# One whole load of the output projection's weights, shared by prompt and sample, in the attention kernel of a hybrid decoder layer

## The reference

```python
q, k, v (two head groups) = rms_norm(x) @ w_in          # 1024 -> 3072
oa = (softmax(q1 k1') - lam * softmax(q2 k2')) v        # 4 heads, 128-wide; sample: over 32 cache pages of 128 keys
oa = rms_norm(oa per head) * (1 - lambda_init)
ob = three dilated windows, combined                    # 8 heads, 64-wide; sample: over a 2048-row state
x  = x + concat(oa, ob) @ w_out                         # 1024 x 1024, for the prompt AND for the samples
x  = x + (silu(h @ w_gate) * (h @ w_up)) @ w_down       # h = rms_norm(x), 1024 -> 2816 -> 1024
y  = rms_norm(x)
```

## Time and profile before

| | us |
|---|---|
| median of 3 runs | 1243.67 (1239.3 to 1248.49) |
| the profiled execution | 1240.77 |
| its span, first to last instruction | 1238.9 |
| PE busy in it | 1020.4 (82%) |
| DVE busy | 564.7 (46%) |
| ACT busy | 419.4 (34%) |
| POOL busy | 249.4 (20%) |

### The profile page before, as it was taken

How to read it: one execution, slowest core, us unless ns; L and a number is a source line. 1 busy time by engine, 2 the same in 40 slices (tenths; PEclk the granted TensorE clock), 3 DMA queues, 4 the chain that set the end, 5 groups by cost and what they waited for, 6 DMA issues and landing times.

```text
span 1238.9 us, 29111 instructions
## 1 busy us (share of the span) xinstructions
PE 1020.4 (82%) x11290; PEld 896.7 (72%) x11290; DVE 564.7 (46%) x1367; ACT 419.4 (34%) x908; POOL 249.4 (20%) x107
## 2 busy tenths in 40 slices
PE   4969898887777787666656766799999999999994
PEld 3868787776655555444434544599999999999994
DVE  4489666774588999632223411423233232300002
ACT  5544443462254465431304111232222222221112
POOL 2312111211000001010101000133333333434340
PEclk8989998999978998888777865799999999999997
DMA  8689999999999996897574797557777776665542
GB/s 274 207 268 303 305 349 345 340 342 302 360 321 320 333 322 220 265 273 222 157 218 154 212 307 228 195 207 250 252 253 253 253 251 225 237 229 205 195 148 77
DMA packets 209648, 315.11 MB, mean 254 GB/s; under 512 B 14529, under 2 KB 119362, under 8 KB 208002
## 3 DMA queue, kind: packets, MB, share of 16 engines
q1 hardware_dynamic: 209538, 313.63, 75.5%
HBM read 306.50 MB, written 73.92 MB: 307 GB/s over the span
## 4 chain that ended last, share of the span: by engine, by line
PE 53%; DMA 13%; DVE 11%; SPq 11%; issue 7%; ACT 4%; DVEq 0%; ACTq 0%
PE ps L1147 34%; SPq L609 5%; PE ps L865 5%; PE ps L1082 4%; DMA v_ring<-in_cache_v_diff 4%; DMA o_raw<-in_w_out 4%; SPq L600 3%; PE ps L1045 3%; DMA k_ring<-in_state_v_win 3%; DVE kt_sb L1736 3%; PE ps L1003 2%; DVE feat L1635 1%; ACT rot L1271 1%; DMA k_ring<-in_state_k_win 1%; ACT q_st L1407 1%
## 5 line engine op out<-in xcount | busy, mean ns | idle before, releaser
L1736 DVE STREAM_TRANSPOSE kt_sb<-k_ring 128x512 f32<-128x512 f32 x336 | 216.9, 685 | 93.2 <-PE ps L1045 56.8
L827 POOL TENSOR_TENSOR c_lo<-c_raw,c_hi 128x1024 fp32r<-128x1024 f32 (+1 forms) x60 | 156.9, 2614 | 378.7 <-ACT c_hi L1495 378.7
L1495 ACT ACTIVATE c_hi<-c_raw 128x1024 fp32r<-128x1024 f32 (+1 forms) x60 | 68.8, 1147 | 316.2 <-PE ps L1147 262.6
L1147 PE MATMUL ps<-h_lo,c_hi 128*128 128x288 f32 x704 | 152.0, 297 | 0.0
L1147 PE MATMUL ps<-h_hi,c_hi 128*128 128x288 f32 x704 | 150.1, 295 | 1.9 <-DVE h_lo L1612 1.9
L1147 PE MATMUL ps<-h_hi,c_lo 128*128 128x288 f32 x704 | 150.7, 295 | 0.0
L1082 PE MATMUL ps<-v_ring,pt_sb 128*32 128x128 f32 (+1 forms) x2560 | 98.6, 301 | 62.5 <-DMA v_ring<-in_cache_v_diff 45.2
L1082 PEld LDWEIGHTS ps<-v_ring,pt_sb 128*32 128x32 f32 (+1 forms) x2560 | 76.0, 120 | 79.9 <-issue 60.3
L865 PE MATMUL ps<-h_hi,w_hi 128*128 128x288 f32 x384 | 126.3, 329 | 4.0 <-POOL w_lo L784 2.1
L865 PE MATMUL ps<-h_lo,w_hi 128*128 128x288 f32 x384 | 116.2, 303 | 0.0
L865 PE MATMUL ps<-h_hi,w_lo 128*128 128x288 f32 x384 | 116.1, 302 | 0.0
(11 more groups left out here) (165 smaller groups left out, 1519.5 us busy)
## 6 DMA issues: line engine op xcount, KB each, us to landing
k_ring<-in_cache_k_diff SPq DMA_DIRECT2D x256, 256.0 KB, 5.2
v_ring<-in_cache_v_diff SPq DMA_DIRECT2D x256, 256.0 KB, 5.1
out_k_win_sample<-in_state_k_win SPq DMA_DIRECT2D x32, 1020.0 KB, 7.6
out_v_win_sample<-in_state_v_win SPq DMA_DIRECT2D x32, 1020.0 KB, 7.9
k_ring<-in_state_k_win SPq DMA_DIRECT2D x80, 256.0 KB, 5.3
v_ring<-in_state_v_win SPq DMA_DIRECT2D x52, 256.0 KB, 7.5
w_raw<-in_w_in SPq DMA_DIRECT2D x24, 512.0 KB, 5.9
c_raw<-in_w_gate SPq DMA_DIRECT2D x22, 512.0 KB, 3.8
```

What stands on the lines that cost most here:

```text
L827: nc.gpsimd.tensor_tensor(c_lo[:, j, 0:width], c_raw[:, j, 0:width], c_hi[:, j, 0:width].bitcast(F32), ALU.subtract).then_inc(w_lo_done, 1)
L1147: last = nc.tensor.matmul(main_ps[:, 2 * bank + c, 0:HALF], wt[:, j, w], act[:, k0 + k, c * HALF:(c + 1) * HALF], start=start and k == 0 a ...
L1495: nc.scalar.activation(c_hi[:, j, 0:width], c_raw[:, j, 0:width], ACT.Copy).then_inc(w_hi_done, 1)
L1736: V.transpose(kt_sb[:, i, :], k_ring[:, i, :]).then_inc(kt_done, 1)
```

## The change

`wo_sb` becomes two halves of 512 output columns, each [128, 8, 512], and is loaded once, in eight loads of 512 KB (256 segments of 2 KB each): half 0 at pieces ATTN + 8, + 16, + 24 and + 32, half 1 at OUT, + 2, + 4 and + 6. The prompt's splits read their 128 columns out of it, and the samples' product reads it later. `o_raw`, its eight loads and the second whole load go away. As half 0 lies where `oT` was, `oT` moves to the place of `kT`, and `mix_l` is then written over `oT` itself. The four waits for stores out of region OR, which SP had ahead of its first chunk, go to POOL ahead of its first `o_lo`; SP's wait on `w_used` before each chunk goes, as do its waits on `mix_lo`. ACT waits for four or eight loads instead of for one chunk, and still for `w_used`.

```diff
--- before.py
+++ after.py
@@ -352,6 +352,7 @@
         q_s = at("q_s", [P, KT, NS], Q0 + 32768)
         k_s = at("k_s", [P, KT, NS], Q0 + 34816)
         mix_h = at("mix_h", [P, KT, SEQ], Q0, F32R)
+        oT = at("oT", [P, KT, SEQ], Q0 + 16384)
         mix_l = at("mix_l", [P, KT, SEQ], Q0 + 16384, F32R)
         h2_hi = at("h2_hi", [P, KT, NT], Q0, F32R)
         h2_lo = at("h2_lo", [P, KT, NT], Q0 + 18432, F32R)
@@ -365,10 +366,9 @@
         R0 = region(36864)
         h_hi = at("h_hi", [P, KT, NT], R0, F32R)
         h_lo = at("h_lo", [P, KT, NT], R0 + 18432, F32R)
-        oT = at("oT", [P, KT, SEQ], R0)
         prob = at("prob", [P, 4, 2, SEQ], R0 + 16384)
         sub_sq = at("sub_sq", [P, 2, SEQ], R0 + 32768)
-        wo_sb = at("wo_sb", [P, KT, D], R0)
+        wo_sb = at("wo_sb", [P, 2, KT, 512], R0)
 
 
         VO = region(2048)
@@ -378,7 +378,6 @@
         ks = at("ks", [NS, 512], OR)
         k_stage = at("k_stage", [P, 2, 4, P], OR + 2048)
         rot = at("rot", [P, NT], OR + 6144)
-        o_raw = at("o_raw", [P, 2, D], OR)
         o_lo = at("o_lo", [P, 2, D], OR, F32R)
         KR = region(16384)
         k_ring = at("k_ring", [P, 8, 512], KR)
@@ -655,11 +654,9 @@
                     sp.dma_start(dst.rearrange("l o (b p) h d -> p (l o b) (h d)", p=P),
                                  v_tok[:, :, 512 * s:512 * s + 512]).then_inc(done, 16)
 
-            def out_chunk(n):
-
-                m = n - 24
-                sp.dma_start(o_raw[:, m % 2, :].rearrange("p (k c) -> p k c", c=P), w_out[:, :, m * P:(m + 1) * P])\
-                    .then_inc(w_landed[m % 2], 16)
+            def load_w_out(half, k):
+
+                sp.dma_start(wo_sb[:, half, k:k + 2, :], w_out[:, k:k + 2, 512 * half:512 * half + 512]).then_inc(wo_in, 16)
 
             def main(p):
 
@@ -682,22 +679,15 @@
                     sp.dma_start(lw[:, :], consts[:, C_LW:C_LW + WPAGES * 32]).then_inc(lw_in, 16)
                 if p == ATTN + 2:
                     store_group(3)
-                if p == ATTN + 8:
-                    sp.wait_ge(y_free, Y_NO["g", 3] + 1)
-                    sp.wait_ge(k_stored[0], 16 * 4)
-                    sp.wait_ge(k_stored[1], 16 * 4)
-                    sp.wait_ge(ks_stored, 16 * (1 + DB))
-                    out_chunk(24)
-                    out_chunk(25)
+                if p - ATTN in (8, 16, 24, 32):
+                    load_w_out(0, (p - ATTN) // 4 - 2)
                 if p == ATTN + 71:
                     sp.wait_ge(pv_done, UNITS)
                     sp.wait_ge(v_stored, 16 * (2 + DB + 1))
                     for blk in range(4):
                         load_x(blk)
-                m, kk = divmod(p - OUT - 5, 4)
-                if 0 <= m < KT - 2 and kk == 0:
-                    sp.wait_ge(w_used, m + 25)
-                    out_chunk(m + 26)
+                if p - OUT in (0, 2, 4, 6):
+                    load_w_out(1, p - OUT)
 
             for p in range(PRE):
                 main(p)
@@ -726,10 +716,6 @@
                             load_values(t + 1, 0)
                         if t >= KSLOTS - 1 and has_v(t + 2):
                             load_values(t + 2, 0)
-                    if KSLOTS <= t < KSLOTS + 4 and i == 5:
-                        sp.wait_ge(mix_lo, KT)
-                        k2 = 2 * (t - KSLOTS)
-                        sp.dma_start(wo_sb[:, k2:k2 + 2, :], w_out[:, k2:k2 + 2, :]).then_inc(wo_in, 16)
                     if (t, i) == (KSLOTS + 4, 0):
                         sp.wait_ge(x_full, X_NO["m", KSLOTS + 1] + 1)
                         sp.dma_start(g_ffn[:, :], ins["norm_ffn_g"].partition_broadcast(P)).then_inc(norm_in[1], 16)
@@ -794,8 +780,16 @@
 
             def out_split(n):
 
+                m = n - 24
+                if m == 0:
+                    pool.wait_ge(y_free, Y_NO["g", 3] + 1)
+                    pool.wait_ge(k_stored[0], 16 * 4)
+                    pool.wait_ge(k_stored[1], 16 * 4)
+                    pool.wait_ge(ks_stored, 16 * (1 + DB))
                 pool.wait_ge(w_hi_done, n + 1)
-                nc.gpsimd.tensor_tensor(o_lo[:, n % 2, :], o_raw[:, n % 2, :], o_hi[n % 2][:, :].bitcast(F32), ALU.subtract)\
+                cols = slice(m % 4 * P, m % 4 * P + P)
+                nc.gpsimd.tensor_tensor(o_lo[:, n % 2, :].rearrange("p (k c) -> p k c", c=P), wo_sb[:, m // 4, :, cols],
+                                        o_hi[n % 2][:, :].bitcast(F32).rearrange("p (k c) -> p k c", c=P), ALU.subtract)\
                     .then_inc(w_lo_done, 1)
 
             def main(p):
@@ -1171,10 +1165,10 @@
             pe.wait_ge(s_evac, KSLOTS)
             pe.wait_ge(z_free[0], UNITS)
             pe.wait_ge(z_free[1], len(Z_NO))
-            pe.wait_ge(wo_in, 16 * 4)
+            pe.wait_ge(wo_in, 16 * 8)
             for k in range(KT):
                 for h in range(2):
-                    last = nc.tensor.matmul(O[NS * h:NS * h + NS, :], oT_s[:, k, :], wo_sb[:, k, 512 * h:512 * h + 512],
+                    last = nc.tensor.matmul(O[NS * h:NS * h + NS, :], oT_s[:, k, :], wo_sb[:, h, k, :],
                                             start=k == 0, stop=k == KT - 1)
             last.then_inc(xs_out, 1)
 
@@ -1378,12 +1372,14 @@
 
             def out_split_hi(n):
 
-                act.wait_ge(w_landed[n % 2], 16 * (n // 2 - 12) + 16)
+                m = n - 24
+                act.wait_ge(wo_in, 16 * 4 * (m // 4 + 1))
                 if n >= 26:
                     act.wait_ge(w_used, n - 1)
                 elif n == 25:
                     act.wait_ge(masked, UNITS)
-                nc.scalar.activation(o_hi[n % 2][:, :], o_raw[:, n % 2, :], ACT.Copy).then_inc(w_hi_done, 1)
+                nc.scalar.activation(o_hi[n % 2][:, :].rearrange("p (k c) -> p k c", c=P),
+                                     wo_sb[:, m // 4, :, m % 4 * P:m % 4 * P + P], ACT.Copy).then_inc(w_hi_done, 1)
 
             def copy_out(m):
 
@@ -1489,7 +1485,7 @@
 
             def c_split_hi(n, j, half, width=D):
 
-                act.wait_ge(w_landed[j], half * 16 - 176)
+                act.wait_ge(w_landed[j], half * 16 - 240)
                 act.wait_ge(w_used, n - 1)
                 act.wait_ge(w_lo_done, n - 1)
                 nc.scalar.activation(c_hi[:, j, 0:width], c_raw[:, j, 0:width], ACT.Copy).then_inc(w_hi_done, 1)
```

## The result

| | before | changed |
|---|---|---|
| median, us | 1245.24 (4 runs, 1239.3 to 1248.49) | 1182.97 (4 runs, 1180.15 to 1192.54) |
| profiled execution, us | 1240.77 | 1180.15 |
| span, us | 1238.9 | 1178.6 |
| mean granted clock | 0.907 | 0.931 |

The ratio is 0.9519, 95% interval 0.9452 to 0.9585. The changed kernel ran in two further sets beside the kernel before: 0.9558 (0.953 to 0.9587) and 0.9541 (0.951 to 0.9572). So it is 4.4 to 4.8% faster; between medians 56 to 62 us.

What follows compares the result with a forecast made beforehand. The prediction took the output projection to be bound by ACT waiting in order for late chunk loads; -46 + 2 + 3 - 10 = -51 us took 1240.8 to 1189.8, stated as 1191, range 1171 to 1211.

Steps and rivals of the forecast that it cites:

- What bounds the kernel: In the output projection, ACT's split waits for a chunk load with the copy behind it; 46.9 us of PE standing still.
- Part 1: Output projection: chunk loads leave the loop, so the stage falls to 108 us, -46 (ends -64 to -32).
- third way: Third estimate of the projection stage: PE's busy 97.9 us and its 8.2 of waiting for value pages make 106.
- opens fully: Rival: only the ACT order held the projection, DMA goes to 324 GB/s, stage 94 us, total 1171; chance 0.14.
- Part 2: Head of the projection: half 1's first load stands ahead of value pages and delays them, +2 us (ends 0 and +8).
- Part 3: Full prompt attention stage, 360 to 440 us: four half 0 loads replace two chunk loads, +3 us (ends 0 and +6).
- Part 4: Slots 44 to 47, where DMAs are full: the second load of w_out goes, -10 us (ends -3 and -15).
- Part 5: `oT` in the place of `kT`, strided split reads, moved waits and ACT's wait for eight loads: said to cost nothing.
- The sum: -46 + 2 + 3 - 10 = -51, from 1240.8 of the profiled execution to 1189.8; stated as 1191 for the median.
- the pages take half: Rival: page loads, asked for later relative to use, take half the gain; projection 122 us (-32), total 1210; chance 0.16.
- The signs: Profile after: `y_prompt` wait near 0, no w_out DMA on chain, slots 14 to 16 us, projection's DMA share above 0.85.

## Why the prediction was right, step by step

**What bounds the kernel.** Right as to the cause, and one sentence too narrow. The prediction named "the order on ACT: `out_split_hi(m + 25)` waits for a chunk that could be asked for only when tile m - 1 was multiplied", and put weight on the copy that stands behind it. The two halves of that sentence were separable, and only the first carries the loss: with the copy ahead, 0.4% was gained; with the chunk asked for early, the projection's whole gain. The 8.27, 2.63 and 3.56 us of the earlier trace rows, counted beside the 32.4 of the copy, were the sign of it: they are the same stop of ACT seen through other instructions. One reading of the earlier trace rows is too strong: of slices 23 and 24, called full, the second stands at 7 tenths; the window of 705 to 760 at 1.03 carries the point.

**Part 1, -46.** Measured -44.6 (-47.9 in the profiles of both repeats). PE's waits for late work of ACT went as said, from 47.1 to 0.8 us. But its idle time fell by 35.8 only, as its waits for value pages grew by 8.9; and 8.7 us came from the clock, which the sum took as nothing and only the rival "opens fully" counted. These two nearly cancel, so the closeness of the prediction's third way (PE's busy 97.9 and 8.2 of waiting, 106 us) is in part luck: PE was busy 88.6 us and idle 22.3. The slot's 15.06 us of the earlier trace rows was the best guide: 110.9 / 7 = 15.8 after, 15.4 in the repeat. By bytes, 261 GB/s came true against the 266 used.

**Part 2, +2.** The wait at the head was 8.6 us in one execution, 7.4 and 6.7 in two others, against 7.5 before: nothing that can be told. The failed step is "Now the first 0.52 MB load of w_out goes between": it does not. SP's timeline of the changed kernel (in the last section) has the loads of x, then four value pages, those that PE stops for, then a key page, and only then half 1. The prediction put the load one position too early in SP's stream. What stands ahead of the late pages are the loads of x, in both kernels, and with these moved the wait fell from 7.4 to 2.5 us. The rule of the Trainium skill weighed there ("DMA: Bandwidth & Descriptors", section "Queues, rings and completion order"), that a DMA engine takes the descriptors of a ring in order, was put at +8 on the same wrong order. The fall of the wait with x moved agrees with it.

**Part 3, +3.** Not seen. Slots 22 to 36 took 204.9, 207.7 and 203.7 us in the changed kernel against 206.5. The scatter of 4 us between executions is larger than the term; 0 is as good.

**Part 4, -10.** Measured -11.6 by the two profiles, 7.6 to 10.0 by putting the load back. Right in size and place. Moving the load instead of dropping it gave 3 to 4.

**Part 5, nothing.** Right. By tile `wo_sb`, ACT's and POOL's strided reads took as long as the contiguous ones of the earlier trace rows:

```profile
L659 SPq DMA_DIRECT2D wo_sb<-in_w_out x8: 427/494/6044, 356.4 to 565.0; - x8
L1381 ACT ACTIVATE o_hi<-wo_sb x8: 1048/1056/1067, 531.0 to 614.3; 128x1024 fp32r<-128x1024 f32 x8
L791 POOL TENSOR_TENSOR o_lo<-wo_sb,o_hi x8: 2342/2381/2850, 532.2 to 615.4; 128x1024 fp32r<-128x1024 f32 x8
```

1056 ns each on ACT in both kernels, 2381 against 2356 on POOL. `oT` in the place of `kT` added no wait that the stages show: slots 22 to 36, where it is written, took 203.7 to 207.7 us against 206.5.

**The sum.** -51 against -60.3 between the two profiled executions, and against 56 to 62 between medians. By stage the 9.3 us between them are, but for rounding: 3.5 before slot 22, which the change doesn't touch and which went back in the repeats (slot 22 at 341.0 and 339.2); 4.6 in slots 22 to 36 (-1.6 for +3); 0.6 in the projection (-44.6 for -46 + 2); 1.6 in the last stage; less 0.8 at the end. So no stage hides a missing term, and more than a third of the difference is scatter. The step from 1189.8 to 1191 is a slip of its own: the 2.9 us between the profiled execution and the median would give 1192.7. The rival "the pages take half" had the right thing late next, pages, but its stage was to fall by 32 us only; PE's waits for pages grew by 9 us, and the stage fell by 44.6.

**The signs.** They came as named, but for two: the projection's DMA share is 0.83, just short of 0.85, and w_out is not quite off the chain that ended last. None of its transfers is on it, but SP's issues of half 1 are, with 6.04, 2.65 and 0.55 us; what this means is told in the last section.

## What to carry to other kernels

A double buffer that is refilled only when its last user is done gives the load just one tile of time, and an in-order engine that waits for it passes the lateness to all it has behind, whichever instruction that happens to be. Changing that order moved the wait here, asking two tiles earlier removed it. Count the idle time of one engine under all its releasers before you name the one to move. Bytes taken out of a stage whose DMAs are full were worth 8 to 10 us here, of the 13.3 that their transfer takes; the same bytes moved to the stage before gave 3 to 4.

## What the runs showed of the hardware

Two things were not expected. The first is that one issue on SP's queue can itself take long. The first load of half 1 held SP's queue for 6.04 us, against a median of 0.49 for the eight, just after 2.1 MB of x and five pages (1.3 MB) had been issued. The timeline of SP's queue in the changed kernel:

```profile
530.35 2.11 SPq L560 DMA_DIRECT2D x<-in_x_prompt  x4
533.41 3.07 SPq L608 DMA_DIRECT2D v_ring<-in_cache_v_diff  x4
536.52 1.58 SPq L599 DMA_DIRECT2D k_ring<-in_state_k_win  x1
538.16 6.04 SPq L659 DMA_DIRECT2D wo_sb<-in_w_out  x1
545.16 3.02 SPq L608 DMA_DIRECT2D v_ring<-in_cache_v_diff  x4
```

The other four value pages of the slot stand behind it. The two repeats of the changed kernel have 5.70 and 5.50 us at this place. It isn't the load of w_out, nor its size, that makes this issue long. In the kernel before, and in the changed one with half 1 late, a value page of 256 KB has this place in SP's stream, and its issue took 4.85 and 4.58 us, against a median of 0.60. With the four loads of x spread out, the first load of half 1 took 0.42 behind the same five pages, and no issue of these slots took more than 2.85. So the length isn't that of the load held; it goes with what was issued just before, here 2.1 MB of x ahead of five pages. A second place agrees: in the kernel before, a value page issued at 562.85, with no x ahead of it but 2.1 MB of pages and chunk in the 6 us before, took 4.00 us. By what rule an issue is held, and from how many bytes, no run shows.

The second is what the clock gave back. With the same 1185 products in the projection stage, PE's busy time fell from 97.4 to 88.6 us as the mean granted clock rose from 0.78 to 0.88: where idle stops were taken out of PE's stream, a fifth of the gain (8.7 of 44.6 us) came from the clock. In the two repeats PE's busy time there was 84.2 and 86.7 us at 0.92 and 0.91, of a gain of 47.9. That agrees with the rule of the Trainium skill named in the prediction ("TensorE: Matmul & The Clock Gate", section "What's actually happening"), by which activity lifts the clock from its resting level.
